# Orders of work in the latent and the local attention of a four-layer encoder trunk on one core

## The reference, cut to what matters

```
def _mla(h, ...):                       # latent attention, 8 heads
    c_q, c_kv, k_rope = split(h @ w_in)         # 384, 256, 64 columns
    q = rmsnorm(c_q) @ w_uq                     # per head 128 plain + 64 rotary
    k_nope, v = rmsnorm(c_kv) @ w_ukv           # per head 128 + 128
    s = (q_nope @ k_nope.T + rope(q_rope) @ rope(k_rope).T) * scale
    o = softmax(mask(s, chunks of 64)) @ v      # queries in blocks of 128
    return o @ w_o
def _swa(h, ...):                       # local attention, 16 query heads, 4 key heads
    q, k, v = split(h @ w_in + b_in)            # heads of 64, rotary on 16 of them
    s = q @ k.T / 8                             # a chunk of 64 sees itself and the one before
    o = softmax([s, sink])[..., :-1] @ v
    return o @ w_o + b_o
for i in range(4):
    x = x + mixer[i % 3](rmsnorm(x))
    x = x + relu(rmsnorm(x) @ w1)**2 @ w2
return rmsnorm(x)
```

## Time and profile before

| | us |
|---|---|
| median of 3 runs (lowest, highest) | 2088.23 (2086.99, 2089.04) |
| the profiled execution | 2088.25 |
| its span, first to last instruction | 2086.4 |
| busy: TensorE, VectorE, ScalarE, GpSimd | 2060.7, 1153.1, 827.1, 207.8 |
| moved by DMA | 191.29 MB, mean 92 GB/s |

### The profile page before, as it was taken

The page is one execution under the profiler, slowest core; times in us unless marked ns, Lnnn a source line. Parts: engine busy times, 40 slices in busy tenths (PEclk is TensorE's granted clock), DMA queues, the critical chain, the costliest instruction groups (busy, mean ns, idle before and its releaser), DMA issues.

```text
span 2086.4 us, 25172 instructions
## 1 busy us (share of the span) xinstructions
PE 2060.7 (99%) x9800; PEld 1697.4 (81%) x9800; DVE 1153.1 (55%) x1395; ACT 827.1 (40%) x1180; POOL 207.8 (10%) x262
## 2 busy tenths in 40 slices
PE   8999999999999999999999999999999999999998
PEld 6788888888878888888888788888887888888887
DVE  6775544344787744444578654344476756434444
ACT  6564322223466423232356432232345644132233
POOL 6102000000200200004031200000321011000000
PEclk9999999999999999999999999999999999999999
DMA  6222332323322232332322233323231123232331
GB/s 184 63 67 68 104 101 91 100 93 99 107 75 100 94 100 94 97 101 92 104 78 68 87 98 98 100 91 102 93 104 57 61 71 101 92 100 94 97 101 41
DMA packets 121777, 191.29 MB, mean 92 GB/s; under 512 B 16448, under 2 KB 35776, under 8 KB 121696
## 3 DMA queue, kind: packets, MB, share of 16 engines
q1 hardware_dynamic: 116848, 185.78, 27.9%
q0 software_dynamic: 2432, 3.28, 0.7%
q10 hardware_dynamic: 2416, 1.12, 0.2%
HBM read 184.78 MB, written 2.10 MB: 90 GB/s over the span
## 4 chain that ended last, share of the span: by engine, by line
PE 90%; DVE 5%; ACT 3%; issue 1%; DMA 1%; SPq 0%; POOL 0%; DVEq 0%; ACTq 0%
PE psum L557 28%; PE psum L559 28%; PE psum L558 28%; PE psum L866 1%; DVE w_lo L1249 1%; ACT arena L2243 1%; PE psum L975 1%; PE psum L839 1%; DVE small L1568 0%; ACT arena L2231 0%; DMA x<-in_x 0%; PE psum L1078 0%; ACT w_hi L2018 0%; PE psum L1094 0%; PE psum L1108 0%
## 5 line engine op out<-in xcount | busy, mean ns | idle before, releaser
L1249 DVE TENSOR_TENSOR w_lo<-w_raw,w_hi 128x1024 fp32r<-128x1024 f32 x343 | 422.9, 1238 | 790.5 <-ACT w_hi L2018 790.0
L2018 ACT ACTIVATE w_hi<-w_raw 128x1024 fp32r<-128x1024 f32 x343 | 362.3, 1061 | 957.0 <-PE psum L559 956.9
L557 PE MATMUL psum<-h_hi,w_hi 128*128 128x512 f32 x1384 | 546.1, 395 | 0.7 <-DVE arena L1825 0.7
L559 PE MATMUL psum<-h_hi,w_lo 128*128 128x512 f32 x1384 | 538.8, 389 | 0.0
L558 PE MATMUL psum<-h_lo,w_hi 128*128 128x512 f32 x1384 | 538.6, 389 | 0.0
L557 PE MATMUL psum<-u_hi,w_hi 128*128 128x512 f32 x1320 | 516.6, 391 | 1.7 <-DVE u_lo L1448 1.4
L559 PE MATMUL psum<-u_hi,w_lo 128*128 128x512 f32 x1320 | 513.9, 389 | 0.0
L558 PE MATMUL psum<-u_lo,w_hi 128*128 128x512 f32 x1320 | 513.7, 389 | 0.0
L557 PEld LDWEIGHTS psum<-h_hi,w_hi 128*128 128x128 f32 x1384 | 259.9, 188 | 57.9 <-issue 3.6
L558 PEld LDWEIGHTS psum<-h_lo,w_hi 128*128 128x128 f32 x1384 | 259.9, 188 | 56.3 <-issue 3.6
L559 PEld LDWEIGHTS psum<-h_hi,w_lo 128*128 128x128 f32 x1384 | 259.8, 188 | 54.3
(11 more groups left out here) (262 smaller groups left out, 1441.9 us busy)
## 6 DMA issues: line engine op xcount, KB each, us to landing
w_raw<-in_mlp_w SPq DMA_DIRECT2D x256, 512.0 KB, 3.7
w_raw<-in_mla_w_o SPq DMA_DIRECT2D x16, 512.0 KB, 3.5
w_raw<-in_lru_w_in SPq DMA_DIRECT2D x16, 512.0 KB, 4.1
w_raw<-in_swa_w_in SPq DMA_DIRECT2D x12, 512.0 KB, 3.9
w_raw<-in_mla_w_ukv SPq DMA_DIRECT2D x8, 512.0 KB, 4.5
w_raw<-in_lru_w_out SPq DMA_DIRECT2D x8, 512.0 KB, 3.5
w_raw<-in_swa_w_o SPq DMA_DIRECT2D x8, 512.0 KB, 3.6
w_raw<-in_mla_w_in SPq DMA_DIRECT2D x7, 512.0 KB, 4.1
```

The lines of the kernel that those rows point to most:

```text
L557: nc.tensor.matmul(out, stat[0], mov[0], start=start, stop=False, skip_group_check=skip)
L559: return nc.tensor.matmul(out, stat[1], mov[0], start=False, stop=stop, skip_group_check=skip)
L1249: nc.vector.tensor_tensor(w_lo[:, to], w_raw[:, to], exact(w_hi[:, to]), ALU.subtract).then_inc(w_ready, 1)
L2018: nc.scalar.activation(w_hi[:, to], w_raw[:, to], ACT.Copy).then_inc(w_hi_done, 1)
```

## The change

The arithmetic and the number of matmuls, splits, copies and transfers stay as they are; their order changes.

In latent attention, TensorE lays the first half of pair 0's values ahead of the spreading of the key scales, `rope_queries(1)` ahead of head 0's scores, and both halves of pair 1's values around head 0's transposes. VectorE and ScalarE take weight splits, key conversions (`key_lo`), `query_raw(1)`, `values(n)` and `out_hi` in another order, with their number unchanged. In local attention ScalarE takes the norm's root ahead of the rotary tables; three splits move; VectorE does the rest of the head before (`head_lo`) behind the normalising of heads 1 to 6. At the end, TensorE lays three tiles instead of two of output head 6 ahead of head 7's transposes, and the first six products of the second output group (tile 2, chunks 0 and 1) between head 7's weighted values and the last output head; `square_group` leaves those out and doesn't claim their area again.

```diff
--- before.py
+++ after.py
@@ -585,7 +585,7 @@
-def square_group(areas, hi, lo, ready, before_unit=None, halfway=None, last=False):
+def square_group(areas, hi, lo, ready, before_unit=None, halfway=None, last=False, laid=()):
@@ -616,7 +616,10 @@
                     halfway()
-                claim(areas[1])
+                if not laid:
+                    claim(areas[1])
+            if kp == 0 and (kk, m) in laid:
+                continue
             mm = tile(kk, m)
@@ -895,20 +898,20 @@
     keys(0)
+    values(0, 0, 2)
     key_scales()
-    values(0, 0, 2)
     values(0, 1, 2)
     nope_queries(1)
+    rope_queries(1)
     scores(0)
-    rope_queries(1)
     keys(1)
+    values(1, 0)
     transposes(0)
-    values(1, 0)
+    values(1, 1)
     weighted(0)
     scores(1)
-    values(1, 1)
     nope_queries(2)
@@ -1132,6 +1135,15 @@
+    def first_of_second_group():
+        next_unit_ready(1)
+        claim(3)
+        wh, wl = unit(1)
+        for kk in range(2):
+            at = slice(kk * T + 2 * P, kk * T + 3 * P)
+            product(bank(3, 0), (wh[:, at], wl[:, at]), (UHI[kk], ULO[kk]), kk == 0, False)
     query(0)
@@ -1162,13 +1174,14 @@
     out(5)
-    out(6, (0, 1))
+    out(6, (0, 1, 2))
     transposes(7)
-    out(6, (2, 3))
+    out(6, (3,))
     weighted(7)
     jobs["swa", "before out"] |= {name: c.now(name) for name in ("psum_done", "area2", "area3", "area4")}
+    first_of_second_group()
     out(7)
-    square_group((2, 3), UHI, ULO, anything)
+    square_group((2, 3), UHI, ULO, anything, laid=((0, 2), (1, 2)))
@@ -1593,22 +1606,21 @@
     key_lo(0)
-    split(1)
     query_lo(1)
+    split(1)
...
     normalised(0)
+    query_rope(1)
     keys(1)
-    query_rope(1)
     query_rope_lo(1)
-    key_lo(1)
-    split(1)
     head_lo(OHI[0], OLO[0])
...
     normalised(1)
+    key_lo(1)
+    split(2)
     query_lo(2)
-    split(1)
     head_lo(OHI[1], OLO[1])
@@ -1616,14 +1628,13 @@
     query_rope_lo(2)
-    key_lo(2)
-    split(1)
     head_lo(OHI[2], OLO[2])
...
     normalised(3)
+    key_lo(2)
+    split(2)
     query_lo(3)
-    split(1)
     head_lo(OHI[3], OLO[3])
@@ -1631,20 +1642,25 @@
     query_rope_lo(3)
-    key_lo(3)
-    split(2)
     head_lo(OHI[4], OLO[4])
...
     normalised(5)
+    split(1)
+    key_lo(3)
+    split(1)
+    head_lo(OHI[5], OLO[5])
+    largest(6)
+    normalised(6)
     split(2)
-    head_lo(OHI[5], OLO[5])
-    for i in (6, 7):
-        largest(i)
-        normalised(i)
-        split(1)
-        head_lo(OHI[i], OLO[i])
-    split(1)
+    head_lo(OHI[6], OLO[6])
+    largest(7)
+    normalised(7)
+    split(1)
+    head_lo(OHI[7], OLO[7])
+    split(2)
     c.n |= jobs["mla", j, "before out"]
@@ -1908,15 +1923,17 @@
             rotate(i + 1)
-        if i >= 1:
+        else:
             head_lo(UHI[i - 1], ULO[i - 1])
...
         normalised(i, 1)
+        if 1 <= i < KC - 1:
+            head_lo(UHI[i - 1], ULO[i - 1])
         if i + 3 < KC:
...
     head_lo(UHI[KC - 1], ULO[KC - 1])
-    split(2)
+    split(3)
     c.n |= jobs["swa", "before out"]
@@ -2266,59 +2283,65 @@
     query_rope_hi(0)
-    split(1)
     values(0, 2)
     query_hi(1)
+    split(1)
+    query_raw(1)
     exponentials(0)
-    query_raw(1)
     turned(0)
+    query_rope_hi(1)
     key_hi(1)
-    query_rope_hi(1)
-    split(1)
     out_hi(0)
+    values(1)
     exponentials(1)
-    values(1)
+    split(1)
     query_hi(2)
     turned(1)
+    split(1)
     query_raw(2)
-    split(1)
     out_hi(1)
...
     key_hi(2)
+    out_hi(2)
     values(2)
-    split(1)
-    out_hi(2)
     exponentials(3)
+    split(1)
     query_hi(3)
     turned(3)
+    split(1)
     query_raw(3)
-    split(1)
     out_hi(3)
...
     key_hi(3)
+    out_hi(4)
     values(3)
+    exponentials(5)
+    split(1)
+    turned(5)
+    split(1)
+    out_hi(5)
+    exponentials(6)
+    split(1)
+    turned(6)
+    split(1)
+    out_hi(6)
+    exponentials(7)
+    split(1)
+    turned(7)
+    out_hi(7)
     split(2)
-    out_hi(4)
-    exponentials(5)
-    turned(5)
-    split(2)
-    out_hi(5)
-    for i in (6, 7):
-        exponentials(i)
-        turned(i)
-        split(1)
-        out_hi(i)
-    split(1)
     c.n |= {name: jobs["mla", j, "before out"][name] for name in ("psum_done", "tensor_unit")}
@@ -2445,8 +2468,8 @@
     split(3)
+    column_root()
     rotary_tables(1)
-    column_root()
     split(1)
@@ -2487,18 +2510,17 @@
     key_bias()
+    split(1)
     act.wait_ge(area_free[1], jobs["v"])
     nc.scalar.activation(m["v_back"][CHUNK:P, :], m["v"][0:CHUNK, :], ACT.Copy)
+    query_bias(0)
     nc.scalar.activation(m["v_back"][0:CHUNK, 256:], m["v"][CHUNK:P, 0:3 * 256], ACT.Copy)
-    query_bias(0)
-    split(1)
     act.wait_ge(k_rotated, 1)
...
     query_bias(1)
-    split(1)
     query_bias(2)
```

More of the change, by code:

```diff
@@ L1595, in mla @@
                 key_lo(0)
+                query_lo(1)
                 split(1)
-                query_lo(1)
                 largest(0)
                 normalised(0)
+                query_rope(1)
                 keys(1)
-                query_rope(1)
                 query_rope_lo(1)
-                key_lo(1)
-                split(1)
                 head_lo(OHI[0], OLO[0])
@@ L2268, in mla @@
                 query_rope_hi(0)
-                split(1)
                 values(0, 2)
                 query_hi(1)
+                split(1)
+                query_raw(1)
                 exponentials(0)
-                query_raw(1)
                 turned(0)
+                query_rope_hi(1)
                 key_hi(1)
-                query_rope_hi(1)
+                out_hi(0)
+                values(1)
+                exponentials(1)
                 split(1)
-                out_hi(0)
-                exponentials(1)
-                values(1)
                 query_hi(2)
                 turned(1)
+                split(1)
                 query_raw(2)
-                split(1)
                 out_hi(1)
@@ L2292, in mla @@
                 key_hi(2)
+                out_hi(2)
                 values(2)
+                exponentials(3)
                 split(1)
-                out_hi(2)
-                exponentials(3)
                 query_hi(3)
                 turned(3)
+                split(1)
                 query_raw(3)
-                split(1)
                 out_hi(3)
```

## The result

| | kernel before | changed kernel |
|---|---|---|
| device time, median of 4 runs | 2087.99 us (2086.99 to 2089.04) | 2075.40 us (2074.29 to 2076.14) |
| profiled execution, span | 2086.4 us | 2072.5 us |
| ratio | 1 | 0.9939, 95% interval 0.9928 to 0.9951 |

12.6 us less; 15.1 were forecast. A second set of four runs gave 2074.61 against 2087.00, 12.4 less.

The account below looks back on a forecast made before the run. TensorE, busy 99% of the span, was taken as the bound. Latent attention's 10.4 us and local attention's 4.7 sum to 15.1, so 2088.25 - 15.1 = 2073.1 us, range 2070.8 to 2078.0.

Parts of the forecast that it names:

- the price of a wait: Whole program: TensorE is the bound, and each of its waits costs its idle time plus 0.16 us.
- rival (a): TensorE's waits: each costs only what the idle column shows, so the time is 2076.4 us; chance 0.10.
- Key scales and head 0: Latent attention: key-scale wait goes, rope products fill the wait before head 0's scores; gain 1.9 and 1.6 us by layer.
- Heads 1, 3 and 5: Latent attention: conversion and splits move behind the normalising, so the six transpose waits go; gain 6.1 us.
- rope behind the values copy: Latent head 1: rope products no longer wait for ScalarE's value copies, now ahead of the exponentials; 0.38 twice, 0.8 us.
- Local front: Local attention's start: earlier norm root removes waits at the spread, head 0's scores and query 3; 2.4 us, at worst 1.2.
- rival (c): Swapped rows come late: front gives 1.2 us less, each latent layer's query swap up to 0.6; 2075.5 us; chance 0.08.
- Local heads: Local attention's heads: the last head's rest moves behind the normalising; gain 0.6 us, and 0.1 at head 0.
- Tail: Local attention's end: output products fill TensorE's waits around head 7; 0.36 + 1.37 - 0.1 = 1.6 us.
- (b): ScalarE becomes late for weighted values, slipping 0.5 us at ten heads; 5 us return, 2078 us; chance 0.12.
- (d): Splits waiting for weights hold up ScalarE's softmax; loads 2 us late at ten heads give 2093 us; chance 0.05.
- (e): VectorE isn't in time at latent attention's odd heads: 6.1 us stay, output units cost 1 more; 2080 us; chance 0.04.

Follow-up runs that it names:

- tensor-order-only kernel: Changed kernel with VectorE's and ScalarE's old order restored in latent attention, TensorE's new order kept; 2088.74 us beside 2087.74 for the kernel before (ratio 1.0002).

## Why the prediction was right, and where not

- *Bound, and the price of a wait* (idle plus 0.16): right. By rival (a) latent attention would have given 10.4 - 10 x 0.16 = 8.8; 10.4 came.
- *Key scales and head 0* (1.9 and 1.6): the sum was right, the steps were not. The wait at the key scales was counted as gone; it moved to the nope products (0.92 and 0.87 lost), whose buffer VectorE frees only by converting the first keys. In return head 0's scores have no wait at all. The buffer that TensorE needs next was the edge left out of the walk.
- *Heads 1, 3 and 5* (6.1) and *rope behind the values copy* (0.8): right; no transposes of latent attention wait.
- *Local front* (2.4): the step that failed, 0.70 instead of 2.5 with head 0's 0.1. The spread's 0.66 and query 3's 0.75 came. Head 0's scores gained nothing (they lost 1.19, before 1.03), since the key swaps landed after up to 3.6, where 2.4 was taken; and the second half of head 0's transposes lost 0.47, as the rotation of query 1 waited 0.60 for its own swap. This is rival (c) in its place. In size it had 1.2 for the front, where 1.8 went missing, and 0.6 more for query swaps in latent attention, which lost nothing; that its 2075.5 is so near the measured 2075.4 is luck. And its mechanism was wrong: not the shared port, for which the Trainium skill was cited (SBUF: State Buffer, SBUF: two separate sides), but the load that the moved split sets off; with the load held and the split in place the landings were 2.0 to 2.1, and POOL's issues took 0.5 us each in either case. "A unit that is used 15 us later" was costed by when its split is due, and not by what its slot releases. With 0.70 in its place the sum is 13.3, and the time 2075.0, against the measured 2075.4. The size is not a constant: in the seven traces where the load goes out among the swaps the front gains from 0.15 to 1.1, in the five where it goes out later from 1.6 to 2.0, in none 2.5.
- *Local heads* (0.6): 0.38. *Tail* (1.6): 1.82; beginning the group apart cost nothing that shows.
- *Rivals (b), (d), (e)*: behind the start of the program no wait of TensorE for ScalarE, none for a load, none at odd heads.
- *The chip's clock*: untouched in the stages (1.00 in all).

## What to carry to other kernels

A split or copy that frees a slot is also the start of a transfer: when moving it, look at what the queue behind that slot will load and which small transfers, waited for by an engine, are in flight at that moment; here holding one load back by 3 us was worth 1.3, although it met the next small transfers instead. When a wait is removed by new work ahead of it, check the buffer that the engine asks for next. And reorderings of a producer and its consumers are to be judged together: apart they gave half or less than nothing.

## What the hardware showed that was not expected

**Small transfers beside a large one.** The four key-row transfers of 32 KB from one place of the on-chip buffers to another land 2.0 to 2.2 us after their issue in the kernel before and with the load later. When a 512 KB load starts among them the slowest takes 3.6 to 4.0, in each of the seven traces that have the early split and no held load; in the seven others it takes 2.1 or 2.2. The order matters too: with the load going out between the second swap's issue and the third's, the first two of the changed kernel's swaps land after 2.1 and 2.2 us, the two behind it after 3.6. What the two kinds of transfer share isn't shown here, only that the load alone makes the difference.

**Where the runs of one kernel part.** The runs of most kernels here differ by 1 to 3 us, and their mean granted clock, 0.999 or 0.998, doesn't tell them apart (2074.27 and 2076.19 both have 0.998). The traces show two places. One is the start, up to the first changed instruction (see the ledger); the larger one is the end of the program. Up to the end of the last attention stage the two traces of the changed kernel differ by 0.6 (the swaps), at the end of the program by 1.9. In the last 14 us TensorE goes over to one-column products for the final norm and then to transposes, and about there the granted clock falls from 1.00 (2.4 GHz) to half of it. From 2062 to 2068 us, first and second trace (the last columns are the granted clock as a mean of the stretch, DMA share, GB/s):

```profile
2062.00:2068.00 6.00, 5.95 (x39) 5.71 (x38) 3.13 (x10) 2.74 (x5) 0.00 (x0) 0.72 0.34 124
```

```profile
2062.00:2068.00 6.00, 5.70 (x27) 5.70 (x28) 2.54 (x10) 1.54 (x4) 0.00 (x0) 0.53 0.12 43
```

From the last weighted values of the second latent layer to the end it is 391.3 to 391.9 us in nine of the traces and 392.5 to 392.6 in five, whatever was changed in the middle; in exactly those five the first stretch at the lower clock is some 3.4 us longer. That is why a step of 0.6 us is read here from the ledger and not from medians of four. Why the tensor-order-only kernel scatters more, up to 2089.8 at a clock of 0.997, stays open: only its fastest run has a trace.
